# Splitting the last output-projection unit in two, and 64-column modulation sums, in a two-layer hybrid trunk

## The reference

```python
c_act = jax.nn.silu(c)
for l in range(DEPTH):
    mod = (c_act @ ada_w[l] + ada_b[l])[:, None, :]
    sh1, sc1, g1, sh2, sc2, g2 = jnp.split(mod, 6, axis=-1)
    h = rmsnorm(x, norm_mix_w[l]) * (1.0 + sc1) + sh1
    x = x + g1 * hybrid_mixer(h, ...)
    h = rmsnorm(x, norm_ffn_w[l]) * (1.0 + sc2) + sh2
    ffn = swiglu(h, ...) if l % 2 == 0 else moe_swiglu(h, ...)
    x = x + g2 * ffn
return rmsnorm(x, final_norm_w)
```

## Time and profile before

| | us |
|---|---|
| three runs | 1503.07, 1505.87, 1507.31 |
| median | 1505.87 |
| span of the profiled execution, first to last instruction | 1505.1 |
| TensorE busy in the span | 1490.6 |
| VectorE busy | 1299.7 |
| ScalarE busy | 959.8 |
| mean granted TensorE clock, of full speed | 0.994 |

### The profile page before, as it was taken

The page is one execution under the profiler, slowest core; times in us unless marked ns, Lnnn a source line. Parts: engine busy times, 40 slices in busy tenths (PEclk is TensorE's granted clock), DMA queues, the critical chain, the costliest instruction groups (busy, mean ns, idle before and its releaser), DMA issues.

```text
span 1505.1 us, 24325 instructions
## 1 busy us (share of the span) xinstructions
PE 1490.6 (99%) x8505; PEld 1311.0 (87%) x8505; DVE 1299.7 (86%) x1529; ACT 959.8 (64%) x1107; POOL 26.7 (2%) x44
## 2 busy tenths in 40 slices
PE   8999999999999999999999999999999999999997
PEld 7999888999999999888988888888888888888886
DVE  7999787777775799787799999999999999999998
ACT  3636445444544535444588888887878878788885
POOL 0000000000000000000010000000000000000100
PEclk9999999999999999999999999999999999999999
DMA  9956498388995646588399999999999999999993
GB/s 349 341 173 221 151 331 293 103 291 297 377 410 193 210 154 218 174 291 306 109 398 397 410 394 404 372 379 409 363 392 369 382 406 364 393 369 379 411 393 139
DMA packets 210458, 470.89 MB, mean 313 GB/s; under 512 B 16156, under 2 KB 93140, under 8 KB 210388
## 3 DMA queue, kind: packets, MB, share of 16 engines
q1 hardware_dynamic: 206624, 457.27, 83.0%
q0 software_dynamic: 3488, 12.59, 2.1%
q10 hardware_dynamic: 276, 0.09, 0.0%
HBM read 454.69 MB, written 15.21 MB: 312 GB/s over the span
## 4 chain that ended last, share of the span: by engine, by line
PE 94%; DVE 3%; DMA 1%; ACT 0%; issue 0%; DVEq 0%; SPq 0%; ACTq 0%
PE psU L671 68%; PE psA L671 24%; DVE split L2046 1%; PE psA L1155 1%; DMA raw<-in_ada_w_dram 1%; PE psU L1115 0%; DVE adacc L1655 0%; PE psU L1068 0%; PE psA L747 0%; ACT split L1254 0%; DVE adacc L1652 0%; DVE work L1655 0%; DVE merged L1677 0%; DVE xT L2027 0%; DVE work L1652 0%
## 5 line engine op out<-in xcount | busy, mean ns | idle before, releaser
L1254 ACT ACTIVATE split<-raw 128x1024 fp32r<-128x1024 f32 x750 | 781.8, 1061 | 300.0 <-PE psU L671 134.3
L2046 DVE TENSOR_TENSOR split<-raw,split 128x1024 fp32r<-128x1024 f32 x528 | 617.2, 1221 | 22.8 <-ACT split L1254 10.4
L671 PE MATMUL psU<-split,yS 128*128 128x512 f32 x2448 | 564.6, 390 | 0.1
L671 PEld LDWEIGHTS psU<-split,yS 128*128 128x128 f32 x2448 | 458.0, 188 | 94.9 <-DVE split L2046 0.8
L671 PE MATMUL psU<-hS,split 128*128 128x256 f32 x2688 | 331.0, 285 | 0.1
L1507 DVE TENSOR_TENSOR split<-raw,split 128x1024 fp32r<-128x1024 f32 x222 | 264.2, 1219 | 77.3 <-ACT split L1254 76.5
L671 PEld LDWEIGHTS psU<-hS,split 128*128 128x128 f32 x2688 | 326.3, 193 | 1.5 <-issue 1.2
L671 PE MATMUL psA<-split,hidE 128*128 128x512 f32 x1056 | 246.0, 392 | 0.0
L671 PEld LDWEIGHTS psA<-split,hidE 128*128 128x128 f32 x1056 | 196.4, 188 | 40.2
L671 PE MATMUL psU<-split,hS 128*128 128x512 f32 x720 | 168.4, 391 | 0.0
L671 PEld LDWEIGHTS psU<-split,hS 128*128 128x128 f32 x720 | 134.3, 188 | 28.0 <-DVE split L1507 0.4
(11 more groups left out here) (267 smaller groups left out, 824.5 us busy)
## 6 DMA issues: line engine op xcount, KB each, us to landing
raw<-in_moe_w_dram SPq DMA_DIRECT2D x496, 512.0 KB, 5.8
raw<-in_w_in_dram SPq DMA_DIRECT2D x116, 512.0 KB, 6.0
raw<-in_ada_w_dram SPq DMA_DIRECT2D x96, 512.0 KB, 7.8
raw<-in_ffn_w_dram SPq DMA_DIRECT2D x66, 512.0 KB, 8.6
raw<-in_moe_w_dram SPq DMA_DIRECT2D x64, 256.0 KB, 6.2
raw<-in_w_o_dram SPq DMA_DIRECT2D x16, 512.0 KB, 5.5
token_rows<-sc SPq DMA_DIRECT2D x11, 512.0 KB, 13.0
raw<-in_w_br_a_dram SPq DMA_DIRECT2D x8, 512.0 KB, 6.6
```

The source lines that it names most:

```text
L671: return pe.matmul(o, a, b, start=start, stop=stop, skip_group_check=True)
L1254: return act.activation(o, i, ACT.Copy)
L2046: TTN(split[:, slot, 1, :], raw[:, (RAW0 + n) % RAW, :], split[:, slot, 0, :].bitcast(F32), ALU.subtract).then_inc(s_lo, 1)
```

## The change

The fourth unit of the output projection becomes two units of one chunk each. Both of its pieces are taken first; the first new unit runs its 24 matmuls over both pieces, then the second. Both pieces are counted as used in the second unit. ScalarE squares the two chunks apart, and TensorE sums them apart (`stat_chunk`). The scale's eight sums are split around the last chunk's sum of squares: two ahead of it, six behind. VectorE takes the reciprocal ahead of the scale's `modulate`. All modulation sums multiply with 64 columns of ones in place of one, and `modulate` reads every 64th column.

```diff
-        plan += [((l, "wo", j), "D") for j in range(4)]
+        plan += [((l, "wo", j), "D") for j in range(5)]
...
+        elif kind == "wo" and key[-1] == 3:
+            direct += 1
+            signal[key] = ("direct", direct, used)
         elif kind in HEAD_GROUPS or kind == "wo":
-            used += (3, 1, 2, 2)[key[-1]] if kind == "wo" else 2
+            used += (3, 1, 2, 0, 2)[key[-1]] if kind == "wo" else 2
...
-            def stat_pair(bank, count, j):
-
-                pe.wait_ge(s_sq, 4 * (count - 2) + j + 1)
-                for k in range(2):
-                    last = mm(bank[:, 0:T], ones[:, :], sig[:, j, k * T:(k + 1) * T], j == 0 and k == 0,
-                              j == 3 and k == 1)
-                if j == 3:
+            def stat_chunk(bank, n, ch):
+
+                pe.wait_ge(s_sq, SQ_BASE[n] + (ch - 2 if n != 1 else 4))
+                last = mm(bank[:, 0:T], ones[:, :], sig[:, 3, (ch % 2) * T:(ch % 2 + 1) * T], False, ch == KD - 1)
+                if ch == KD - 1:
                     last.then_inc(s_ev, 1)
-                return last
...
                 for k in ks:
-                    last = mm(bank[:, k:k + 1], acc[:, k * P:(k + 1) * P], ones[:, 0:1], True, True)
+                    last = mm(bank[:, k * WIDE:(k + 1) * WIDE], acc[:, k * P:(k + 1) * P], ones[:, 0:WIDE], True, True)
...
-                for j, q in WO_ORDER:
+                for j, q in WO_ORDER[:6]:
...
+                ws = [next_split() for _ in range(2)]
+                for m in range(2):
+                    bank = open_unit((l, "wo", 3 + m))
+                    for q in range(2):
+                        for kk in range(4):
+                            last = tile(bank[:, 0:T], ws[q], 4 * q + kk, kk * 256 + m * P, q == 0 and kk == 0,
+                                        q == 1 and kk == 3)
+                        if m:
+                            last.then_inc(s_used, 1)
+                    if m == 0:
+                        last.then_inc(s_unit, 1)
                 stat_sum(stat, 2 * l)
-                ada_sum(6 * l + 4, scale)
-                stat_pair(stat, 2 * l + 2, 3)
+                stat_chunk(stat, 2 * l, 6)
+                ada_sum(6 * l + 4, scale, range(NORM_KS))
+                stat_chunk(stat, 2 * l, 7)
+                ada_sum(6 * l + 4, scale, range(NORM_KS, KD))
                 ada_sum(6 * l + 3)
...
+                    if second and j == 3:
+                        for m in range(2):
+                            if m:
+                                high_parts(SIGNAL[l, "wo", 4][2] + AHEAD)
+                                act.wait_ge(s_uD, emptied(UNITS, UNIT_AT[(l, "wo", 4)], "D"))
+                            act.activation(sig[:, 3, m * T:(m + 1) * T], xT[:, 6 + m, :], ACT.Square).then_inc(s_sq, 1)
+                    else:
+                        act.activation(sig[:, j, :], xT[:, 2 * j:2 * j + 2, :].rearrange("p a b -> p (a b)"),
+                                       ACT.Square).then_inc(s_sq, 1)
...
                 if second:
-                    low_parts(SIGNAL[l, "wo", 3][2] + AHEAD)
-                    modulate(6 * l + 4)
+                    low_parts(SIGNAL[l, "wo", 4][2] + AHEAD)
                 else:
                     modulate(NORM_SUMS[0])
                 dve.wait_ge(s_eA, emptied(EVENTS, EVENT_AT[(l, "norm2" if second else "norm1")], "A"))
                 link(dve.reciprocal(rstd[:, :], rstd[:, :]))
+                if second:
+                    modulate(6 * l + 4)
                 modulate(6 * l + 3 if second else NORM_SUMS[1])
...
-                for j in range(4):
+                for j in range(5):
                     bank = unit((l, "wo", j))
-                    for m in range(2):
-                        ch = 2 * j + m
+                    for m in range(2 if j < 3 else 1):
+                        ch = 2 * j + m if j < 4 else 7
...
-                        if m:
+                        if m or j > 2:
                             ins.then_inc(s_uD, 1)
```

More of the change, by code:

```diff
@@ L52 @@
 WO_ORDER = [(0, 0), (1, 0), (0, 1), (1, 1), (2, 0), (2, 1), (3, 0), (3, 1)]
+SQ_BASE = [0, 5, 9]
 ADA_B, LB_ROW, NA_ROWS = 0, 96, 104
@@ L81 @@
 NORM_SUMS = [7, 6, 11]
+NORM_KS = 2
 LAST_ROWS = 3
@@ L1026, in dense_ffn @@
                 stat_sum(stat, 1).then_inc(s_used, 1)
-                stat_pair(stat, 3, 3)
+                for ch in (6, 7):
+                    stat_chunk(stat, 1, ch)
                 ada_sum(NORM_SUMS[0], scale, range(5, KD))
@@ L1070, in turn_rows @@
                 last.then_inc(s_unit, 1)
-            pe.wait_ge(s_uD, emptied(UNITS, UNIT_AT[(1, "wo", 3)], "D"))
+            pe.wait_ge(s_uD, emptied(UNITS, UNIT_AT[(1, "wo", 4)], "D"))
             for j in range(3):
@@ L1294, in norm @@
             def norm(l, second):
-                used = SIGNAL[l, "wo", 3][2] if second else FFN_END + NF if l else 0
+                used = SIGNAL[l, "wo", 4][2] if second else FFN_END + NF if l else 0
                 std(early[:, 2 * l + second:2 * l + second + 1], eps[:, :], 1)
@@ L1307, in norm @@
                         act.wait_ge(s_eD, emptied(EVENTS, EVENT_AT[f"down{j // 2}"], "D"))
-                    act.activation(sig[:, j, :], xT[:, 2 * j:2 * j + 2, :].rearrange("p a b -> p (a b)"),
-                                   ACT.Square).then_inc(s_sq, 1)
+                    if second and j == 3:
[7 more added lines that the diff above has]
+                                       ACT.Square).then_inc(s_sq, 1)
                 bank, _ = event((l, "norm2" if second else "norm1"))
@@ L1597, in modulate @@
                 dst = mod[:, l, 8 * part:8 * part + 8]
-                TTN(dst, bank[:, 0:KD], vecs[:, ADA_B + 8 * s:ADA_B + 8 * s + 8],
+                sums = bank[:, 0:KD * WIDE].rearrange("p (m r) -> p m r", r=WIDE)[:, :, 0]
+                TTN(dst, sums, vecs[:, ADA_B + 8 * s:ADA_B + 8 * s + 8],
                     ALU.add).then_inc(s_uD if unit_sum else s_eD, 1)
@@ L1609, in sum_squares @@
             def sum_squares(n):
-                dve.wait_ge(s_sq, 4 * n + 2)
+                dve.wait_ge(s_sq, SQ_BASE[n] + 2)
                 link(TTN(sig[:, 0, :], sig[:, 0, :], sig[:, 1, :], ALU.add))
-                dve.wait_ge(s_sq, 4 * n + 3)
+                dve.wait_ge(s_sq, SQ_BASE[n] + 3)
                 settle()
@@ L1984, in mixer @@
                 settle()
-                unit_done((l, "wo", 3))
+                unit_done((l, "wo", 4))
                 norm(l, 1)
```

## The result

The changed kernel takes 1513.26 us (1512.77 to 1513.95, four runs) against 1505.83 (1503.07 to 1507.31): a ratio of 1.0044, 95% interval 1.0033 to 1.0056. It is slower, and the time lies above the range of the prediction, 1501.0 to 1508.5. Its profiled execution took 1512.77 for a span of 1510.8, so 2.0 us lie around the span. By that the profiled execution of the kernel before, with a span of 1505.1, was itself about 1.2 above its median; the spans differ by 5.7, the medians by 7.4.

What follows compares the result with a forecast made beforehand. TensorE's stream was taken to bound the kernel. At full clock -1.5 - 2.4 + 1.2 = -2.7 us on a median of 1505.9 gave 1503.2; with a fall in one second norm the forecast was 1504.7, range 1501.0 to 1508.5.

Steps and rivals of the forecast that it cites:

- The bound: Whole kernel: TensorE holds 94% of the chain that ended last; only lengthening or stalling its stream moves the end.
- the exceptions: From 753 us VectorE's low parts bound the experts' start; what delays the router delays that start too.
- the split unit: Output projection's end, layer 0: last add begins 0.2 later than 273.02; it and its square end at 274.15.
- The root begins there and not at 276.10: 1.25 earlier: Second norm, layer 0: ScalarE's root starts when the last sum of squares lands, at 274.8.
- The new wait: Second norms: shift's sums wait for the scale's banks until behind the reciprocal; TensorE stands some 1.1 us.
- The clock: At the norms: neither a fall nor a hold at a second norm is fixed; full clock everywhere gives -2.7 us.
- Rival C: Clock falls in both second norms but holds at the first norm: +0.4, 1506.3 us; chance 0.13.
- B: The forecast: clock holds at the first norm and falls in one of two second norms; 1504.7 us, chance 0.38.
- The 64 columns: Modulation sums: nothing taken for their own time; if they hold the clock at layer 1's first norm, -2.4 us.
- Rival E: Layer 1: clock falls behind TensorE's wait, stays down over turns and logits; +8.5 there, 1514.4 us in all; chance 0.06.
- the sign named for it: Layer 1, second norm: over 4 us lost between the projection and the logits.

Runs made afterwards that it cites:

- old_order: Changed kernel with sums and `modulate` back in the order of the kernel before, split unit and 64 columns kept; 1502.6 us, ratio 0.9967.
- root_count: Changed kernel with ScalarE's root waiting for its own event's count alone, the scale's `modulate` still behind the reciprocal; 1507.1 us, ratio 1.0012.
- event_order: Changed kernel with the events planned in the order norm, scale, shift; 1502.2 us, ratio 0.9975.
- cols_only: Kernel before with 64 columns in all modulation sums and nothing else; 1502.9 us, ratio 0.9980.
- scale_first: Changed kernel with the scale's `modulate` put back ahead of the reciprocal; 1503.3 us, ratio 0.9983.
- wait_only: Kernel before with the scale's `modulate` moved behind the reciprocal and nothing else; 1517.6 us, ratio 1.0062.
- one_col: Changed kernel with one column in the modulation sums, as before the change; 1517.6 us, ratio 1.0067.

## Why the prediction was wrong, by its steps

- **The bound, the exceptions and the split unit** stood. The last add begins 0.38 behind the projection's end where it began 0.20 behind before: the delay of 0.2 that was forecast. old_order shows no other cost.
- **"The root begins there and not at 276.10: 1.25 earlier" failed.** I ended the chain at the matmul that makes the root's input and did not ask which count ScalarE waits for. No row of before could show it: there the scale was counted first anyway. The line of code did: `event` waits for the event's own place in the plan. root_count measured 1.18 earlier once the count was right, so the durations were right and a wait was missing. With that one wait gone the time is 1507.1, inside the stated range, though still slower than the kernel before, by a ratio of 1.0012 (1.0004 to 1.0021), where 1.2 us less were forecast. By the medians 6 us, by the ratios 5, hang on this step. They hang on it through TensorE's stand, which the held root makes 2.5 us long in place of 1.2; by itself it costs the 0.53 and 0.70 of event_order.
- **The new wait** was right in place and mechanism and mis-sized for the same reason: 2.47 and 2.57 instead of 1.1. In root_count it was 1.18 and 1.28.
- **The clock** decided more than I allowed. Rival C, a fall in both, had a chance of 0.13; it is what the profile shows. The distances came to 13.41 and 11.39 where C had about 10.5 and 10.0. 1.4 of each is the longer stand. The other 1.5 in layer 0 is an error in the sum: B and C let the fall last "about as long as now" and charged 1.45 for it (283.3 in place of 281.85), but the fall of the kernel before, some 6.8 us from inside 276 to 277 to inside 283 to 284 (the window below), had cost 3.2 by cols_only. The changed kernel's is as long, from inside 279 to 280 to inside 286 to 287, and costs 3.3: its sums and fillers, from start to start, take 2.88 and 4.72 where root_count at full clock took 1.80 and 2.46. Some 0.3 came back, since the rest of the chain was shorter than forecast. So against the kernel before the 2.85 lost in layer 0 is nearly all the stand, and the 4.27 in layer 1 the stand and a fall that the profile before did not have there. C's price of 1506.3, these 4.3, 0.3 missing at the first norm and 1.2 by which the profile before stood over its median make 1512.1. The 1.2 that are left are the 0.7 by which the two profiles differ outside the three norms and the 0.5 by which the profile after lies under its median.

```profile
283.00:284.00 1.00, 1.00 (x7) 0.76 0.00 0
```

- **The 64 columns** were right: -2.1 for -2.4, and a few hundredths for a set of sixteen (1.89 in cols_only against 1.84). I took the fall in layer 0 as given and credited the columns nothing there; the profile of cols_only shows 3.2 us.
- **Rival E** had the right mechanism, TensorE's new wait and a fallen clock behind it, at 1514.4 and 0.06, and the sign named for it, over 4 us lost between the projection and the logits, came (4.27). Its condition came by half: the clock fell ahead of the turns but did not outlast the logits, since it rose inside 740 to 741 and they began at 741.29. That its time lies 1.1 from the measured one is luck: E has no held root, a longer fall in layer 1 and a stand of 1.1.

## What to carry to other kernels

When work is reordered, follow each consumer to the count that it waits for: on a shared counting semaphore the consumer of an event that finishes early still waits for all that were planned ahead of it, and the cure is to reorder the plan with the work. When a small vector operation is moved behind a long one, look for the engine that needs its bank. One-column sums ahead of heavy matmuls are worth trying wider: here 64 columns cost a few hundredths of a microsecond for a set, held the granted clock at 1.00 where no stand of 1.2 us or more followed, and gave 0.2%.

## What the runs showed of the hardware

Sixteen matmul instructions with 64 columns took 1.89 us in cols_only and with one column 1.84 in the kernel before, both at full clock: the columns were nearly free. In cols_only the granted clock stayed at 2.4 GHz behind them at all three norms, where in the kernel before it had fallen to 1.2 GHz behind one column at two of the three.

With 64 columns the clock fell behind a stand of 2.5 us in both layers of the changed kernel and held behind stands of up to 0.5 in scale_first. Behind one of 1.2 in root_count it stayed full in layer 0 and fell in layer 1 of the same execution. The Trainium skill, TensorE: Matmul & The Clock Gate, Part 1 (The HAM clock gate), says that the gate's window runs free and does not restart with the kernel. The two layers of root_count agree with it, as nearly the same stand had either outcome.

In the changed kernel's second norm of layer 1 the clock rose inside 740 to 741, after a stretch at 1.2 GHz that began inside 737 to 738 and held the tail of the sums, 2.6 us of turns (737.74 to the fillers' start at 740.30) and hardly any filler. In root_count it rose inside 734 to 736, at about 734.2 (an estimate from the mean of 0.95), while the turns still ran (732.20 to the fillers' start at 734.50). The Trainium skill, TensorE: Matmul & The Clock Gate, Part 4 (PE-mode transpose), says that transposes do not count as busy in the same way. In these two profiles the turns did not keep the clock down, and the measurement decides. It does not decide for every case: in wait_only and one_col, whose sums have one column, the clock stayed at 1.2 GHz through all the turns, which in wait_only ran from 741.36 to 743.95. This window of wait_only follows them:

```profile
744.00:746.00 2.00, 2.00 (x8) 0.50 0.33 119
```

Whether the turns or the one-column sums ahead of them kept it down there stays open.
